# Expert weights in places of 32 KB, filled by one transfer with two chunks, and identity products behind three chunks of a round

## The reference

```python
def hierarchical_moe(x, g_ffn, w_rg, b_rg, w_re, b_re, w_gate, w_up, w_down):
    ...
    combine = jnp.sum(jax.nn.one_hot(flat_idx, N_EXPERTS, dtype=jnp.float32) * top_w[..., None], axis=1)
    combine = combine.reshape(-1, N_EXPERT_GROUPS, EXPERTS_PER_GROUP).astype(x.dtype)
    out = jnp.zeros_like(xn)
    for g in range(N_EXPERT_GROUPS):
        h = jax.nn.silu(jnp.einsum('nd,edf->nef', xn, w_gate[g])) * jnp.einsum('nd,edf->nef', xn, w_up[g])
        out = out + jnp.einsum('nef,efd->nd', h * combine[:, g, :, None], w_down[g])
    return x + out.reshape(bsz, L, D_MODEL)
```

## Time and profile before

| | |
|---|---|
| median of 3 runs | 1620.34 us (1619.79 to 1622.34) |
| profiled execution, its own time | 1620.38 us |
| span from first to last instruction | 1618.6 us |
| mean granted TensorE clock | 0.958 |
| TensorE matmul busy | 1418.7 us, 88% |
| VectorE, ScalarE busy | 563.1 us, 408.6 us |
| moved by DMA | 544.69 MB, mean 337 GB/s |

### The profile page before, as it was taken

One profiled execution on the slowest core, in us unless ns is written; L12 is line 12 of the kernel. 1 busy time (PEld: TensorE's weight loads), 2 busy tenths in 40 slices (PEclk: granted clock), 3 DMA queues, 4 the chain that ended last, 5 costly groups with the idle time before them and its releaser, 6 DMA issues.

```text
span 1618.6 us, 24633 instructions
## 1 busy us (share of the span) xinstructions
PE 1418.7 (88%) x10019; PEld 932.5 (58%) x10019; DVE 563.1 (35%) x924; ACT 408.6 (25%) x684; POOL 14.4 (1%) x30
## 2 busy tenths in 40 slices
PE   7999999999999999999977878877868867968966
PEld 7999999999999999953322322322312412412411
DVE  5647765554455555542211112112111111201204
ACT  7554344333333344420201101002002002002003
POOL 0100000000000010000000000000000000000000
PEclk9999999999999999999999989889989899989999
DMA  8777445545555659689999999999999999999997
GB/s 334 287 286 260 148 171 182 181 164 194 182 181 180 255 223 349 241 352 426 427 428 428 428 427 425 431 427 426 429 428 426 427 430 426 427 429 427 427 427 315
DMA packets 55470, 544.69 MB, mean 337 GB/s; under 512 B 7265, under 2 KB 7265, under 8 KB 13033
## 3 DMA queue, kind: packets, MB, share of 16 engines
q1 hardware_dynamic: 55282, 544.04, 82.9%
q10 hardware_dynamic: 144, 0.03, 0.0%
HBM read 540.30 MB, written 3.68 MB: 336 GB/s over the span
## 4 chain that ended last, share of the span: by engine, by line
PE 53%; DMA 40%; SPq 5%; DVE 1%; ACT 1%; issue 1%; DVEq 0%; ACTq 0%
DMA ring<-in_expert_chunks 24%; PE bank L1461 13%; PE bank L1462 13%; PE bank L1463 13%; DMA side<-in_expert_chunks 8%; DMA trunk<-in_expert_chunks 4%; SPq L519 4%; PE bank L1853 4%; PE bank L1856 3%; DMA spare<-in_expert_chunks 2%; PE bank L1739 2%; PE bank L1793 1%; DMA ring<-in_dense_units 1%; PE bank L1731 1%; PE bank L1785 1%
## 5 line engine op out<-in xcount | busy, mean ns | idle before, releaser
L933 DVE TENSOR_TENSOR w_lo<-ring,w_hi 128x1024 fp32r<-128x1024 f32 x220 | 259.8, 1222 | 223.0 <-ACT w_hi L666 222.6
L1461 PE MATMUL bank<-xn_hi,w_hi 128*128 128x264 f32 x1120 | 319.0, 285 | 0.0
L1462 PE MATMUL bank<-xn_lo,w_hi 128*128 128x264 f32 x1120 | 317.3, 283 | 0.0
L1463 PE MATMUL bank<-xn_hi,w_lo 128*128 128x264 f32 x1120 | 317.1, 283 | 0.0
L666 ACT ACTIVATE w_hi<-ring 128x1024 fp32r<-128x1024 f32 x220 | 221.1, 1052 | 366.7 <-PE bank L1463 349.5
L1461 PEld LDWEIGHTS bank<-xn_hi,w_hi 128*128 128x128 f32 x1120 | 210.9, 188 | 1.1 <-issue 1.0
L1462 PEld LDWEIGHTS bank<-xn_lo,w_hi 128*128 128x128 f32 x1120 | 211.1, 188 | 0.1
L1463 PEld LDWEIGHTS bank<-xn_hi,w_lo 128*128 128x128 f32 x1120 | 210.0, 187 | 0.0
L1853 PE MATMUL bank<-side,trunk 128*32 128x512 f32 x832 | 115.9, 678 | 52.2 <-DMA side<-in_expert_chunks 51.4
L1739 PEld LDWEIGHTS bank<-trunk,x_all 128*128 128x128 f32 (+1 forms) x672 | 94.4, 194 | 76.7 <-issue 56.8
L878 ACT ACTIVATE side<-bank 128x512 f32<-128x512 f32 x32 | 19.1, 597 | 439.7 <-PE bank L1856 439.7
(11 more groups left out here) (308 smaller groups left out, 1724.0 us busy)
## 6 DMA issues: line engine op xcount, KB each, us to landing
ring<-in_expert_chunks SPq DMA_DIRECT2D x79, 2048.0 KB, 37.8
ring<-in_dense_units SPq DMA_DIRECT2D x109, 1024.0 KB, 4.8
side<-in_expert_chunks SPq DMA_DIRECT2D x48, 2048.0 KB, 42.6
trunk<-in_expert_chunks SPq DMA_DIRECT2D x24, 2048.0 KB, 36.1
spare<-in_expert_chunks SPq DMA_DIRECT2D x16, 2048.0 KB, 30.9
ring<-in_expert_chunks SPq DMA_DIRECT2D x18, 1024.0 KB, 24.6
trunk<-in_expert_chunks SPq DMA_DIRECT2D x16, 1024.0 KB, 44.0
side<-in_expert_chunks SPq DMA_DIRECT2D x16, 1024.0 KB, 44.8
```

Of the source, the lines that this page charges most:

```text
L933: V.tensor_tensor(w_lo[n % 2][:, js, :], raw[n % 2][:, js, :], w_hi[n % 2][:, js, :], ALU.subtract).then_inc(lo_done, 1)
L1461: mm(ps[:, 0:n], w_hi[b][:, j, :], x_hi[:, j, :], start=j == k0, stop=False)
L1462: mm(ps[:, 0:n], w_hi[b][:, j, :], x_lo[:, j, :], start=False, stop=False)
L1463: ins = mm(ps[:, 0:n], w_lo[b][:, j, :], x_hi[:, j, :], start=False, stop=j == k1 - 1)
```

## The change

The expert chunks are joined in pairs. There are five places of 32 KB a partition (`pair`, order in `PAIR_SLOT`), each for the chunks 2q and 2q + 1. In DRAM the two chunks of a pair are laid side by side, partition by partition, so one transfer of 128 rows x 32 KB brings both. The pair's place gets free with the odd chunk of the pair before in it (`FREED_BY`, `AHEAD`). Chunks 22 and 23 stay apart, 23 in halves. In round 0, chunks 0 to 19 are still loaded one by one, each waiting for the chunk ten before; 20 and 21 come as a pair that waits for chunk 15. `spare` is gone (it is now part of `side`), and the gathered tokens `xgT` move from `trunk` to `side`. TensorE waits once for a pair, ahead of its even chunk, except for single chunks. Behind chunks 9, 11 and 13 of every round stand sixteen `stay_busy` products.

```diff
-EARLY = 5
+EARLY = (2, 3, 1, 8, 4)
-SLOT = [9, 4, 5, 7, 6, 1, 0, 3, 2, HALVES] * 2 + [6, 1, 0, 3]
...
+PAIRS = CPR // 2
+PAIR_SLOT = [4, 3, 0, 1, 2] * 2 + [0, 1]
+HIGH_FIRST = (True, False, False, False, True)
+SINGLES = 10
+FREED_BY = {5: 1, 6: 3, 7: 5, 8: 7, 9: 9, 10: 15, 11: 17}
+AHEAD = {0: None, 1: None, 2: 21, 3: 23, 4: None}
...
+        pair = [view(ring, 0, 2 * CHUNK), view(ring, UNIT0, 2 * CHUNK), view(trunk, 0, 2 * CHUNK),
+                view(side, 4096, 2 * CHUNK), view(side, 12544, 2 * CHUNK)]
...
-        xgT = view(trunk, CHUNK + 3 * D, KT, P)
+        xgT = view(side, 0, KT, P)
...
+            def pair_load(q, round_of):
+
+                if q in SP_STEPS:
+                    sp.sem_inc(sp_step, 1)
+                if q < PAIRS - 1:
+                    s = PAIR_SLOT[q]
+                    sp.dma_start(pair[s].rearrange("p (o n) -> p o n", o=1), pair_v[:, q, round_of, :]).then_inc(full[s], 16)
                 else:
-                    sp.dma_start(e_slot[s].rearrange("p (o n) -> p o n", o=1), chunk_v[:, c, round_of, :]).then_inc(full[s], 16)
+                    one_load(2 * q, round_of)
+                    words_of(2 * q + 1, 0, CHUNK // 2, round_of, last_in)
+                    words_of(2 * q + 1, CHUNK // 2, CHUNK, round_of, half_full)
...
-            for c in (7, 8):
-                sp.wait_ge(z_ready, Z_END + c - 8)
-                expert_load(c, slice(0, 1))
-            half_of(9, 0, slice(0, 1), full[HALVES])
-            sp.wait_ge(aux_ready, A_LT + 1)
-            half_of(9, 1, slice(0, 1), full[HALVES])
+            for c in (6, 7):
+                sp.wait_ge(z_ready, Z_END + c - 7)
+                one_load(c, slice(0, 1))
+            one_load(9, slice(0, 1))
...
             with sp.Fori(0, npass) as k:
-                refill(REFILL, k * (ROUNDS * CPR) + CREDIT, slice(0, 1))
-                refill(AHEAD, k * (ROUNDS * CPR) + CREDIT, slice(1, 2))
+                base = k * (ROUNDS * CPR) + CREDIT
+                for c in range(SINGLES, 2 * SINGLES):
+                    sp.wait_ge(e_used, base + (c - SINGLES + 1))
+                    one_load(c, slice(0, 1))
+                for q in (10, 11):
+                    sp.wait_ge(e_used, base + (FREED_BY[q] + 1))
+                    pair_load(q, slice(0, 1))
+                ahead(base, slice(1, 2))
...
-                        pe.wait_ge(full[SLOT[c]], it * slot_fills(c) + expert_full(c))
+                        if c % 2 == 0:
+                            pe.wait_ge(full[PAIR_SLOT[c // 2]], it * round_fills(c // 2) + pair_fills(c // 2))
+                        elif c < 2 * SINGLES:
+                            pe.wait_ge(second_in[c // 2], k * 16 + 16)
+                        elif c == CPR - 1:
+                            pe.wait_ge(last_in, it * 16 + 16)
...
                         ins.then_inc(e_used, 1)
+                        if c in (9, 11, 13):
+                            stay_busy(16, 5)
...
+    for q in range(PAIRS - 1):
+        order = slice(None, None, -1) if HIGH_FIRST[PAIR_SLOT[q]] else slice(None)
+        both = out[:, 2 * q:2 * q + 2][:, order].transpose(0, 2, 1, 3)
+        out[:, 2 * q:2 * q + 2] = np.ascontiguousarray(both).reshape(ROUNDS, 2, P, CHUNK)
```

More of the change, by code:

```diff
@@ L52 @@
 Z_END = Z_O + 16
-EARLY = 5
+EARLY = (2, 3, 1, 8, 4)
 CPR = 24
 CREDIT = 8
-HALVES = 8
-SLOT = [9, 4, 5, 7, 6, 1, 0, 3, 2, HALVES] * 2 + [6, 1, 0, 3]
[L59 to L62, removed]
+PAIRS = CPR // 2
[4 more added lines that the diff above has]
+AHEAD = {0: None, 1: None, 2: 21, 3: 23, 4: None}
+SP_STEPS = (0, 3, 4, 7, 8, 11)
 _n = 0
@@ L226, in branch_kernel, with place, weights @@
         mem_lo = split_part("mem_lo", TRUNK0 + 2 * KT * T, KT * NM).rearrange("p (j t) -> p j t", j=KT)
[L228 to L235, removed]
+        pair = [view(ring, 0, 2 * CHUNK), view(ring, UNIT0, 2 * CHUNK), view(trunk, 0, 2 * CHUNK),
+                view(side, 4096, 2 * CHUNK), view(side, 12544, 2 * CHUNK)]
+        def place(c):
+            s = PAIR_SLOT[c // 2]
+            return s, ((c % 2 == 1) != HIGH_FIRST[s]) * CHUNK
+        def weights(c, jj):
+            s, at = place(c)
+            at += jj * (CHUNK // 2)
+            return pair[s][:, at:at + CHUNK // 2].rearrange("p (e n) -> p e n", e=EPR)
         y = view(side, 2048, 2, 512)
@@ L331, in branch_kernel @@
         smx, snegm, srs = view(small, 224, 1), view(small, 225, 1), view(small, 226, 1)
-        full = [sem(f"slot{i}_full") for i in range(10)]
+        full = [sem(f"pair{i}_full") for i in range(5)]
+        second_in, last_in = [sem(f"second{q}_in") for q in range(SINGLES)], sem("last_in")
         mem_in, x_in, xt_in = [sem(f"mem{i}_in") for i in range(4)], [sem("x0_in"), sem("x1_in")], sem("xt_in")
@@ L383, in lo_after, with pair_fills, round_fills @@
             return lo_done, g * (8 * PIECES) + PIECES * (N_MKV + n + 1)
[L385 to L391, removed]
+        def pair_fills(q):
+            return sum(16 for k in range(q + 1) if PAIR_SLOT[k] == PAIR_SLOT[q])
+        def round_fills(q):
+            return sum(16 for k in range(PAIRS) if PAIR_SLOT[k] == PAIR_SLOT[q])
         units_v = dense_units.rearrange("m p n -> p m n")
         chunk_v = expert_chunks.rearrange("r c p n -> p c r n")
+        pair_v = expert_chunks.rearrange("r (q t) p n -> r q (t p n)", t=2).rearrange("r q (p m) -> p q r m", p=P)
         raw = [view(ring, b * KT * P, KT, P) for b in range(2)]
@@ L527, in _ @@
                     sp.dma_start(lgb[:, NG:36], row(b_re[0].rearrange("g e -> (g e)"), P)).then_inc(router_in, 16)
-                    expert_load(0, slice(0, 1))
+                    one_load(0, slice(0, 1))
                 if n == N_OUT - 4:
@@ L542, in _ @@
                         sp.dma_start(g_row, g_final.rearrange("(o n) -> o n", o=1)).then_inc(gfin_in, 16)
-                    if 3 <= k < 3 + 2 * EARLY and k % 2:
-                        expert_load(k // 2, slice(0, 1))
+                    if 3 <= k < 3 + 2 * len(EARLY) and k % 2:
+                        one_load(EARLY[k // 2 - 1], slice(0, 1))
             sp.wait_ge(aux_ready, A_O + KT - 4)
@@ L548, in _ @@
             residual(KT - 2)
[L549 removed]
+            for half, signal in ((0, half0_full), (1, second_in[2])):
                 sp.wait_ge(*lo_after(N_OUT + 14 + half))
[L551 to L557 removed]
+                words_of(5, half * (CHUNK // 2), (half + 1) * (CHUNK // 2), slice(0, 1), signal)
+            for c in (6, 7):
+                sp.wait_ge(z_ready, Z_END + c - 7)
+                one_load(c, slice(0, 1))
+            one_load(9, slice(0, 1))
             sp.wait_ge(rows_last, 1)
@@ L561, in _, with refill, ahead @@
             npass = sp.value_load(npass_i[0:1, 0:1], min_val=1, max_val=9)
-            def refill(loads, base, of_round):
-                for p, c in loads:
+            def refill(base, of_round):
+                for q, p in FREED_BY.items():
+                    sp.wait_ge(e_used, base + (p + 1))
+                    pair_load(q, of_round)
+            def ahead(base, of_round):
+                for q, p in AHEAD.items():
                     if p is not None:
                         sp.wait_ge(e_used, base + (p + 1))
-                    if c in SP_STEPS:
-                        sp.sem_inc(sp_step, 1)
-                    expert_load(c, of_round)
+                    pair_load(q, of_round)
             with sp.Fori(0, npass) as k:
-                refill(REFILL, k * (ROUNDS * CPR) + CREDIT, slice(0, 1))
-                refill(AHEAD, k * (ROUNDS * CPR) + CREDIT, slice(1, 2))
+                base = k * (ROUNDS * CPR) + CREDIT
[6 more added lines that the diff above has]
+                ahead(base, slice(1, 2))
                 with sp.Fori(1, ROUNDS - 1) as r:
-                    refill(REFILL, k * (ROUNDS * CPR) + r * CPR + CREDIT, bass.ds(r, 1))
-                    refill(AHEAD, k * (ROUNDS * CPR) + r * CPR + CREDIT, bass.ds(r + 1, 1))
-                refill(REFILL, k * (ROUNDS * CPR) + ((ROUNDS - 1) * CPR + CREDIT), slice(ROUNDS - 1, ROUNDS))
+                    refill(k * (ROUNDS * CPR) + r * CPR + CREDIT, bass.ds(r, 1))
+                    ahead(k * (ROUNDS * CPR) + r * CPR + CREDIT, bass.ds(r + 1, 1))
+                last = k * (ROUNDS * CPR) + ((ROUNDS - 1) * CPR + CREDIT)
+                refill(last, slice(ROUNDS - 1, ROUNDS))
                 with sp.If(k < npass - 1):
-                    refill(AHEAD, k * (ROUNDS * CPR) + ((ROUNDS - 1) * CPR + CREDIT), slice(0, 1))
+                    for q, p in AHEAD.items():
+                        if p is not None:
+                            sp.wait_ge(e_used, last + (p + 1))
+                        one_load(2 * q, slice(0, 1))
+                        one_load(2 * q + 1, slice(0, 1))
                 sp.nop()
```

31 lines of the change are left out of this document (12 added, 19 removed).

## The result

The changed kernel takes 1634.9 us (median of 4 runs, 1633.94 to 1636.41) against 1621.2 us for the kernel before on the same chips (4 runs): a ratio of 1.0087, 95% interval 1.0075 to 1.01. It is slower by 13.7 us, inside the range of 1621.5 to 1636 but 5 us more than the 8.4 forecast. The profiled execution took 1634.0 us with a span of 1632.3, so 13.6 us above that of before. The median of the kernel before varied from 1620.3 to 1621.2 us between sets of runs.

The account below looks back on a forecast made before the run. The prediction took the expert stage's unbroken stream of weights as the bound. Fewer packet sets -7.0, a round 0 hole +13.0 and the tail +2.4 made +8.4 us, so 1628.7 us, range 1621.5 to 1636.

Parts of the forecast that it names:

- the second rival: Expert weight stream: rows of 32 KB are no cheaper, only the halvings' 1.1 us is saved, 1634.6 us; chance 13%.
- (a): Expert weight stream: 93 fewer sets of packets (112 against 205) at 0.075 us each, -7.0 us.
- The three cycles a packet: Expert weight stream: the skill's packet cost, estimated at 28 ns a set, 2.6 us for the 93; sum then +12.8 us.
- (b): Round 0: products delay chunk 15's release, so pair (20, 21) loads late and the stream is empty, +13.0 us.
- No second hole: Round 0, chunk 22's refill after chunk 17: flows at 780.9 us, just as the pair ends at 781.4.
- (c): End of last round: chunk 20 arrives together with 21, so the last half chunk starts 2.4 us later.
- both chunks start at that 1595.44: Last round: chunks 20 and 21 start at 1595.44 us, where 21 alone started after a wait before.
- counted the low clock as free: Expert stage: chunks at low clock (3.54 us against 1.92 warm) cost nothing, since the next wait absorbs it.
- The products keep the clock up: Later rounds: chunks take 1.92 instead of 3.54 us, saving time that nobody waits for; cost 0.
- The first (cheap products): Round 0, release of chunk 15: the products cost little there; 1616.7 us if they cost nothing; chance 7%.
- the third (13 us gained): Expert weight stream: the 32 KB rows gain more, -13 us, 1622.7 us; chance 12%.
- the fourth (rows 32 KB apart read slower): Paired chunks: stream at 423 GB/s instead of 427.5, +8 us in place of the gain, 1644 us; chance 5%.

Follow-up runs that it names:

- experiment 5: The changed kernel with a pair's two chunks left apart in DRAM, two rows of 16 KB per partition instead of one of 32 KB: 1636.91 us, ratio 1.0102.
- experiment 6: The changed kernel, products kept, with chunks 20 and 21 of round 0 loaded singly, waiting for chunks 14 and 15: 1629.18 us, ratio 1.0061.
- experiment 1: The changed kernel without the sixteen identity products behind chunks 9, 11 and 13: 1620.35 us, ratio 0.9998.
- experiment 4: The changed kernel with twelve identity products behind chunk 15 of every round instead of those behind 9, 11 and 13: 1618.62 us, ratio 0.9983.
- experiment 2: The kernel before with only the sixteen identity products behind chunks 9, 11 and 13 added: 1629.91 us, ratio 1.0054.
- experiment 7: The changed kernel without loop products, chunks 0 to 15 paired in rounds 1 to 7, chunks 16 to 23 single in every round: 1615.21 us, ratio 0.9965.

## Why the prediction was right, and where it was off

The measured +13.7 us lies inside the range, 1.1 us from its upper end, and above the 1625 to 1633 us that the forecast itself was given. The time alone would point to the second rival (rows of 32 KB no cheaper, 1634.6 us), which is refuted below: the forecast's saving and its hole were there, and 5.4 us more in the tail.

**(a) Sets of packets: right.** Forecast 0.075 us a set and 7.0 us in all. The round fell from 117.73 to 116.73 us, 13 sets, 0.077 each; seven rounds make 7.0 us and round 0 a little more. Rows of 32 KB do cost one packet (experiment 5). The three cycles a packet of the Trainium skill ("DMA: Bandwidth & Descriptors", "Why small descriptors are slow (HBM only)"), 28 ns a set by the prediction's estimate, are too low for this stream by a factor of 2.7; the measured 0.075 us decides.

**(b) The hole: right in place, cause and size, one detail missed.** Forecast: pair issued at 769.65 us, measured 769.09; blocks of 4.0 us, measured 3.76; empty windows at 760 to 770. "No second hole" failed: the step had 0.5 us to spare and assumed the full clock for chunk 16 of round 0, which ran at 3.53 us. In sum the stream ends 5.8 us later by the landing of pair (16, 17) plus 29.3, where -7.0 + 13.0 says 6.0. The windows agree: both holes together lose 12.5 us where 13.0 was forecast for one, so the second hole happens to make up for blocks that were shorter than forecast. The order of causes also differs from the forecast: with the second hole it is chunk 22's wait for chunk 17 that sets the later stream, and the joined wait of (20, 21) matters little (experiment 6).

**(c) The tail: the term that was mis-sized.** Forecast +2.4, found +7.8. The order of arrival is worth 2.3 us (experiments 1 and 4), as worked out. The step "both chunks start at that 1595.44" took for granted that TensorE would be ready then. The chain from pair (16, 17) to there, by the prediction's own durations, has to fit into the time in which two pairs arrive and has almost no slack: pairing 16 and 17 made it start 4.9 us later as well. With the low clock in chunks 16 and 17 it is 5.8 us longer, and 5.5 of that reach the end (7.8 less 2.3). I had counted the low clock as free because a DMA wait absorbs it. That holds as long as a wait follows, and none follows behind the last pairs.

"The products keep the clock up" was also too simple. They do so in the 32 us up to the end of chunk 14 (granted clock 0.99 on average over rounds 2 to 6, against 0.83 without the products in experiment 1), where nothing depends on it, and there are none between chunks 15 and 16, where the end of the kernel does.

**Rivals.** The first (cheap products) is refuted by experiments 1 and 2, the second (no gain from 32 KB) by experiment 5, the third (13 us gained) and the fourth (rows 32 KB apart read slower) by the round of 116.73 us. The fourth's 423 GB/s came from no row; the rate measured is 431.

## What to carry to other kernels

Where a stream of loads is the bound, filler work on the engine that frees the buffers is free only where that engine waits. In the first round, in which it runs ahead of the stream, each microsecond in front of a release can become a microsecond without data; and the last round has no later wait to absorb anything. So work out both ends by themselves, and let the last pieces arrive one by one, even where big transfers are better in the middle (experiment 7). Filler that stands only behind the last release that a load waits for should cost the stream nothing; no run here had it there.

## What the runs showed of the hardware that I had not expected

- The fixed cost of a packet in a full stream of 16 KB rows is 9 ns (0.075 us for eight), and a row of 32 KB pays it once: 0.83 us of a 117.56 us round for 88 packets an engine. Fewer completions alone gave nothing measurable.
- The level of the clock after a wait is not the same from round to round or run to run. After the same 3.4 us of idle time ahead of chunk 16, the changed kernel had chunk 17 at full clock in one round (1.92 us) and at the low one in the next (3.40 at 1591.16). At the end of the kernel this is worth up to 5.5 us, and the runs of the kernel without products spread over 6.4 us where those of the kernel with twelve products behind chunk 15 spread over 2.2 and the 13 runs of the kernel before, on the chip of the kernel without products, over 3.2.

```profile
1465.10 3.28 PE L1885 MATMUL bank<-ring,side 128*32 128x512 f32 x16 [3.39 <-DMA ring<-in_expert_chunks]
...
1471.48 1.92 PE L1885 MATMUL bank<-ring,side 128*32 128x512 f32 x16
```
